# A first projection unit whose first 128 tokens are multiplied in fp32 from the loaded weights

## The reference

```
h = rms_norm(x, g_mix_pre)
proj = h @ w_in                       # q | k | v | u, 1024 columns each
attn = dilated_mixture_attention(q, k, v)
pool = multiscale_pool(u, w_pool, pool_scale)
x = x + rms_norm(concat(rms_norm(attn), rms_norm(pool)) @ w_out, g_mix_post)
x = x + rms_norm(square(relu(rms_norm(x, g_ffn_pre) @ w_up)) @ w_down, g_ffn_post)
```

## Time and profile before

| | us |
|---|---|
| median of 3 runs | 2038.19 |
| lowest and highest | 2036.93, 2038.52 |
| the profiled execution | 2039.06 |
| its span | 2037.3 |
| TensorE busy | 2018.1 |
| VectorE busy | 1228.1 |
| ScalarE busy | 930.5 |
| GpSimd busy | 122.1 |

### The profile page before, as it was taken

How to read it: one execution, slowest core, us unless ns; L and a number is a source line. 1 busy time by engine, 2 the same in 40 slices (tenths; PEclk the granted TensorE clock), 3 DMA queues, 4 the chain that set the end, 5 groups by cost and what they waited for, 6 DMA issues and landing times.

```text
span 2037.3 us, 29067 instructions
## 1 busy us (share of the span) xinstructions
PE 2018.1 (99%) x10042; PEld 1712.4 (84%) x10042; DVE 1228.1 (60%) x1386; ACT 930.5 (46%) x1224; POOL 122.1 (6%) x178
## 2 busy tenths in 40 slices
PE   8999999999999999999999999999999999999998
PEld 6888888888888888888888888888888888888886
DVE  5775657655665565565576646676556655655654
ACT  6445657434443443443564456563433443443442
POOL 1820011000000000000100000200000000000000
PEclk9999999999999999999999999999999999999999
DMA  7565355655665565665466543565565565566553
GB/s 269 166 217 170 118 177 175 200 203 168 201 206 169 194 197 184 207 201 190 165 218 199 182 155 134 176 196 187 189 200 189 180 205 189 171 209 212 174 199 132
DMA packets 196258, 380.57 MB, mean 187 GB/s; under 512 B 11888, under 2 KB 14048, under 8 KB 195552
## 3 DMA queue, kind: packets, MB, share of 16 engines
q1 hardware_dynamic: 196000, 379.15, 56.1%
q10 hardware_dynamic: 192, 0.54, 0.1%
HBM read 377.55 MB, written 2.10 MB: 186 GB/s over the span
## 4 chain that ended last, share of the span: by engine, by line
PE 94%; DMA 2%; DVE 2%; issue 1%; ACT 1%; POOL 0%; DVEq 0%; POOLq 0%; SPq 0%; ACTq 0%
PE acc_pair L451 24%; PE acc_pair L410 18%; PE acc_pair L412 18%; PE acc_pair L411 18%; PE acc_pair L455 12%; DMA raw<-in_w_in 1%; DVE w_lo L1049 1%; PE acc_pair L584 1%; PE acc_pair L545 1%; PE o_bank L613 1%; DVE h_both L1103 1%; DMA raw<-in_w_up 0%; ACT w_hi L744 0%; PE t_bank L595 0%; PE t_bank L570 0%
## 5 line engine op out<-in xcount | busy, mean ns | idle before, releaser
L1049 DVE TENSOR_TENSOR w_lo<-raw,w_hi 128x1024 fp32r<-128x1024 f32 x704 | 858.2, 1235 | 419.2 <-ACT w_hi L744 400.9
L744 ACT CAST w_hi<-raw 128x1024 fp32r<-128x1024 f32 x704 | 730.1, 1053 | 584.1 <-PE acc_pair L412 243.2
L451 PE MATMUL acc_pair<-h_both,w_hi 128*128 128x512 f32 x2176 | 548.1, 393 | 0.8 <-ACT proj L802 0.8
L410 PE MATMUL acc_pair<-w_hi,f_hi 128*128 128x512 f32 x1280 | 502.0, 392 | 0.0
L412 PE MATMUL acc_pair<-w_hi,f_lo 128*128 128x512 f32 x1280 | 498.4, 389 | 0.0
L411 PE MATMUL acc_pair<-w_lo,f_hi 128*128 128x512 f32 x1280 | 498.2, 389 | 0.0
L451 PEld LDWEIGHTS acc_pair<-h_both,w_hi 128*128 128x128 f32 x2176 | 391.0, 189 | 71.0 <-ACT proj L802 1.7
L455 PEld LDWEIGHTS acc_pair<-h_both,w_lo 128*128 128x128 f32 x2176 | 296.9, 190 | 21.2
L455 PE MATMUL acc_pair<-h_both,w_lo 128*128 128x256 f32 x2176 | 303.4, 282 | 0.0
L412 PEld LDWEIGHTS acc_pair<-w_hi,f_lo 128*128 128x128 f32 x1280 | 240.3, 188 | 50.2
L411 PEld LDWEIGHTS acc_pair<-w_lo,f_hi 128*128 128x128 f32 x1280 | 240.4, 188 | 49.1
(11 more groups left out here) (157 smaller groups left out, 738.1 us busy)
## 6 DMA issues: line engine op xcount, KB each, us to landing
raw<-in_w_up SPq DMA_DIRECT2D x256, 512.0 KB, 4.7
raw<-in_w_down SPq DMA_DIRECT2D x256, 512.0 KB, 4.8
raw<-in_w_in SPq DMA_DIRECT2D x128, 512.0 KB, 4.9
raw<-in_w_out SPq DMA_DIRECT2D x64, 512.0 KB, 5.1
w_pool_s<-in_w_pool SPq DMA_DIRECT2D x2, 1024.0 KB, 9.0
post_row<-in_g_mix_post SPq DMA_DIRECT2D x2, 1024.0 KB, 7.9
post_row<-in_g_ffn_post SPq DMA_DIRECT2D x2, 1024.0 KB, 7.5
out<-x SPq DMA_DIRECT2D x8, 256.0 KB, 2.3
```

Source lines behind the costliest of these rows:

```text
L410: pe.matmul(bank[:, :], xh, wh, start=begin and k == 0, stop=False)
L451: mm = pe.matmul(acc_pair[b][:, m, :], w_hi[:, slot, col:col + P], x_both.rearrange("p s n -> p (s n)"), start=begin and k == 0, stop=end ...
L744: act.copy(w_hi[:, half * PAIRS + p, :], raw[:, p, :]).then_inc(hi_made, 1)
L1049: dve.tensor_tensor(w_lo[:, slot, :], raw[:, p, :], w_hi[:, slot, :].bitcast(F32), ALU.subtract).then_inc(lo_made, 1)
```

## The change

For the first layer's first unit only:

- The first 128 tokens (`first_tokens`) are multiplied as 16 fp32 matmuls of 512 columns, from `h_f` (x turned and multiplied by the gain in fp32, by VectorE) and the loaded weights. It needs neither w_hi nor w_lo. The other 128 tokens (`second_tokens`) are multiplied as before, with `others_turn` ahead of their last pair.
- All eight pairs of weights are loaded without a wait, four into `raw` and four into `raw_b`. x is loaded in seven pieces. All these transfers are issued by SyncE, in the order in which they are needed. The loads of the second unit's first half wait for `lo_made` and for `raw_used`.
- `h_hi` of the first tokens becomes one copy for each piece on ScalarE, `h_lo` one subtraction on VectorE, in a new order among the casts and splits. h_hi and h_lo of the first tokens are still needed by later units.
- TensorE makes ten transposes of the identity ahead of the first gains and six behind the first turn of x, whose result isn't used.

```diff
-            load_half(w_in, 0, 0, 0, 0)
-            sp.dma_start(x[:, 1, :], x_rows[1]).then_inc(x_loaded[2], 16)
+            load_x(0, 0, c_cols(0))
+            load_first(0, 0)
+            load_x(1, 0, c_cols(1))
+            load_first(1, 0)
+            load_first(2, 0)
+            load_x(2, 0, c_cols(2))
+            load_first(3, 0)
+            load_first(0, 1)
+            load_x(3, 0, c_cols(3))
+            load_first(1, 1)
+            load_first(2, 1)
+            load_x(4, 1, c_cols(0))
+            load_first(3, 1)
+            load_x(5, 1, c_cols(1))
+            load_x(6, 1, slice(2 * CH, D))
...
+                    for p in range(PAIRS):
+                        sp.wait_ge(lo_made, RAW + p + 1)
+                        sp.wait_ge(raw_used, p + 1)
+                        sp.sem_inc(raw_loaded[p], 16)
+                        load_half(w_in, 0, 0, 3 * HALF_W, 2, (p,), False)
+                    load_half(w_in, 0, HALF_W, 3 * HALF_W, 3)
...
+            def idle_turns(n):
+
+                for j in range(n):
+                    pe.transpose(o_bank[:, h_cols(j % 4)], ident[:, :], ident[:, :])
+
             pe.wait_ge(ident_made, 2)
+            idle_turns(10)
             pe.wait_ge(gains_loaded, 16)
...
-            h_turns(0, 0, (0, 1))
+            h_turns(0, 0, (0,))
+            idle_turns(6)
...
+            def first_tokens():
+
+                pe.wait_ge(acc_free[0], 1)
+                for s in range(RING):
+                    half, p = s // PAIRS, s % PAIRS
+                    src, loaded = ((raw, raw_loaded), (raw_b, raw_b_loaded))[half]
+                    pe.wait_ge(loaded[p], 16)
+                    pe.wait_ge(h_f_ready, s // 2 + 1)
+                    for k in range(2):
+                        mm = pe.matmul(acc_bank[0][:, :], h_f[:, 2 * s + k, :],
+                                       src[:, p, c_cols(k)], start=(s, k) == (0, 0),
+                                       stop=(s, k) == (RING - 1, 1))
+                    if half == 0:
+                        mm.then_inc(raw_used, 1)
+                    if s in (0, 2, 4, 6):
+                        h_turns(0, 0, (s // 2 + 1,))
+                mm.then_inc(acc_done, 1)
+
+            def second_tokens():
+
+                h_turns(0, 0, (5,))
+                for half in range(2):
+                    for p in range(PAIRS):
+                        if (half, p) == (0, 1):
+                            h_turns(0, 0, (6, 7))
+                        if (half, p) == (1, 3):
+                            others_turn()
+                        pe.wait_ge(lo_made, half * PAIRS + p + 1 + RAW)
+                        pe.wait_ge(h_lo_made, h_pair(0, 0, 4 + 2 * half + p // 2) + p % 2 + 1)
+                        pair(1, p, half, half, h_hi, h_lo, 8 * half, acc_bank[1],
+                             half == 0, half == 1, 0)
...
+            def h_first(c):
+
+                dve.wait_ge(tb_done[c % 2], c // 2 + 1)
+                g = G_MIX + 4 * c
+                dve.tensor_tensor(h_f[:, 4 * c:4 * c + 4, :],
+                                  t_bank[c % 2][:, :].rearrange("p (k n) -> p k n", k=4),
+                                  gain[:, g:g + 4, None].to_broadcast([P, 4, P]), ALU.mult
+                                  ).then_inc(h_f_ready, 1)
...
+            h_first(0)
             split_lo(0, 0, (0,))
-            h_chunks(0, 0, (1,))
-            split_lo(0, 0, (1, 2, 3))
-            h_chunks(0, 0, (2,))
+            h_first(1)
+            split_lo(0, 0, (1,))
+            h_first_lo(0)
+            split_lo(0, 0, (2,))
+            h_first(2)
+            split_lo(0, 0, (3,))
+            h_first_lo(1)
             split_lo(1, 1, (0,))
-            h_chunks(0, 0, (3,))
+            h_first(3)
             split_lo(1, 1, (1,))
-            dve.wait_ge(x_loaded[2], 16)
+            h_first_lo(2)
+            h_first_lo(3)
+            for n in range(4):
+                dve.wait_ge(x_loaded[n], 16)
             dve.sem_inc(x_ready, 4)
             h_first_unit(0, 0, 0, False)
```

More of the change, by code:

```diff
@@ L194, in build @@
     junk = at("junk", [P, CH], F32, r_qkv + 4 * T * CH)
+    raw_b = at("raw_b", [P, RAW, 2 * CH], F32, r_acc)
+    h_f = at("h_f", [P, KT, P], F32, r_qkv + 8 * T * CH)
     act_f = at("act_f", [P, T, CH], F32, r_qkv)
@@ L243, in build @@
     ones_made, warm_done = sem("ones_made"), sem("warm_done")
-    x_loaded = [sem(f"x_loaded{n}") for n in range(3)]
+    x_loaded = [sem(f"x_loaded{n}") for n in range(7)]
     raw_loaded = [sem(f"raw_loaded{p}") for p in range(RAW)]
+    raw_b_loaded = [sem(f"raw_b_loaded{p}") for p in range(RAW)]
+    raw_used, h_f_ready = sem("raw_used"), sem("h_f_ready")
     pool_w_loaded = sem("pool_w_loaded")
@@ L312, in _, with load_x, load_first, load_half @@
             x_rows = x_in[0].rearrange("(t p) d -> t p d", p=P)
[L313 to L319, removed]
+            def load_x(n, t, cols):
+                sp.dma_start(x[:, t, cols], x_rows[t][:, cols]).then_inc(x_loaded[n], 16)
+            def load_first(p, half):
+                dst, loaded = ((raw, raw_loaded), (raw_b, raw_b_loaded))[half]
+                row = half * HALF_W + p * 2 * P
+                src = w_in[0:1, row:row + 2 * P, 0:CH]
+                sp.dma_start(dst[:, p, :].rearrange("p (k c) -> p k c", k=2),
+                             src.rearrange("a (k p) c -> p (a k) c", p=P)
+                             ).then_inc(loaded[p], 16)
+            def load_half(w, l, row, col, hu, which=range(PAIRS), held=True):
+                for p in which:
+                    if held:
+                        sp.wait_ge(lo_made, hu * PAIRS + p + 1)
                     src = w[ld(l, 1), ld(row + p * 2 * P, 2 * P), ld(col, CH)]
@@ L466, in h_turns @@
                     t, c = i // CHUNKS, i % CHUNKS
-                    pe.wait_ge(x_ready, l * 16 + 8 * h + i + 1)
-                    if i >= 2:
+                    if l or h:
+                        pe.wait_ge(x_ready, l * 16 + 8 * h + i + 1)
+                    else:
+                        pe.wait_ge(x_loaded[min(i, 6)], 16)
+                    if (l, h) == (0, 0) and i in (2, 3, 4, 5):
+                        pe.wait_ge(h_f_ready, i - 1)
+                    elif i >= 2:
                         pe.wait_ge(h_lo_made, h_pair(l, h, i - 1))
@@ L503, in others_turn @@
                              ).then_inc(gains_turned, 1)
+            def first_tokens():
[26 more added lines that the diff above has]
+                             half == 0, half == 1, 0)
+            first_tokens()
+            second_tokens()
             for l in range(DEPTH):
@@ L508, in _ @@
                 xg0 = XG_SLOTS + l * XG_LAYER
[L510 to L520, removed]
+                if l > 0:
+                    unit(hu0, a0, h_hi, h_lo, h_first_unit(l, 0))
                 def spread_rstd(n, p):
@@ L741, in split_hi @@
                 for p in which:
-                    act.wait_ge(raw_loaded[p], hu * 16 + 16)
+                    src = raw
+                    if isinstance(hu, int) and hu == 1:
+                        src = raw_b
+                        act.wait_ge(raw_b_loaded[p], 16)
+                    else:
+                        act.wait_ge(raw_loaded[p], hu * 16 + 16)
                     act.wait_ge(w_used, hu * PAIRS + p + 1)
-                    act.copy(w_hi[:, half * PAIRS + p, :], raw[:, p, :]).then_inc(hi_made, 1)
+                    act.copy(w_hi[:, half * PAIRS + p, :], src[:, p, :]).then_inc(hi_made, 1)
             def h_hi_pair(bank, g, dst):
@@ L1048, in split_lo @@
                     slot = half * PAIRS + p
-                    dve.tensor_tensor(w_lo[:, slot, :], raw[:, p, :],
+                    src = raw_b if isinstance(hu, int) and hu == 1 else raw
+                    dve.tensor_tensor(w_lo[:, slot, :], src[:, p, :],
                                       w_hi[:, slot, :].bitcast(F32), ALU.subtract
@@ L1140, in _, with h_first, h_first_lo @@
                             ).then_inc(gains_ready, 1)
-            dve.wait_ge(x_loaded[0], 16)
-            dve.sem_inc(x_ready, 2)
             dve.wait_ge(gain_ready, 1)
-            dve.wait_ge(x_loaded[1], 16)
-            dve.sem_inc(x_ready, 2)
-            h_chunks(0, 0, (0,))
-            split_lo(0, 0, (0,))
-            h_chunks(0, 0, (1,))
-            split_lo(0, 0, (1, 2, 3))
-            h_chunks(0, 0, (2,))
+            def h_first(c):
+                dve.wait_ge(tb_done[c % 2], c // 2 + 1)
[4 more added lines that the diff above has]
+                                  ).then_inc(h_f_ready, 1)
+            def h_first_lo(c):
+                dve.wait_ge(h_hi_made, 2 * c + 2)
+                part = slice(4 * c, 4 * c + 4)
+                dve.tensor_tensor(h_lo[:, part, h_cols(0)], h_f[:, part, :],
+                                  h_hi[:, part, h_cols(0)].bitcast(F32), ALU.subtract
+                                  ).then_inc(h_lo_made, 2)
+            h_first(0)
+            split_lo(0, 0, (0,))
```

(17 more changed lines are left out.)

16 lines of the change are left out of this document (8 added, 8 removed).

## The result

The changed kernel takes 2041.81 us (median of 19 runs, 2040.37 to 2042.82), the kernel before 2038.52 us in the same measurement. The ratio is 1.0015, 95% interval 1.0009 to 1.0022: 3.3 us slower, with a forecast of 3.8. The profiled execution took 2041.83 us with a span of 2040.0, 2.8 and 2.7 more than before.

The account below looks back on a forecast made before the run. TensorE, busy 99% of the span, was taken as the bound, with a nearly level path through VectorE. Plus 3.6 us for the late small gains and 0.2 for the clock gave plus 3.8: 2042.0 us, range 2039.6 to 2044.8.

Parts of the forecast that it names:

- The start: First matmul of the first unit: starts at 6.5 us instead of 10.59, 4.1 us sooner.
- third rival: First loads in one queue start slower, first weights landing at 8.1: plus 5.4 us, 2043.6; chance 0.1.
- The fp32 price: First tokens' fp32 matmuls: 0.87 us each, sixteen taking 13.9 us against 10.9 for 48 split ones, 3.0 more.
- VectorE's stall: Before the first split pair, TensorE waits from 22.6 to 24.7 us for VectorE's low part of h: 2.1 us.
- Turn 3: Turn of x in the first unit where VectorE's last stall starts; its end was forecast at 16.5 us.
- the path: From VectorE's wait through second-unit low parts, loads, casts, squares and root to the projection: TensorE resumes at 53.2 instead of 49.62.
- The deciding term: VectorE waits for the small gains' turn before the second unit's low parts: free at 35.5 instead of 31.89, 3.6 us later.
- The fourth rival: VectorE's wait for the small gains does not decide, so the kernel is not slower: 2034.9 us; chance 0.08.
- ledger of TensorE alone: TensorE's own work in the first unit: done at 34.6 instead of 37.95, so minus 3.3 us.
- The idle transposes: Assumed to raise TensorE's clock ahead of the first unit's matmuls, leaving a cost of only 0.2 us.
- second rival: Idle transposes leave the clock low until 10.2 us, losing 1.8 instead of 0.2: plus 5.4, 2043.6 us; chance 0.29.
- The stated bounds: Forecast case's start (6.2 or 7.3) and fp32 price move it by -0.5 to +1.1: 2041.2 to 2043.2 us.

Follow-up runs that it names:

- e7: Changed kernel with one swap in ScalarE's order, the cast of the sixth pair of weights ahead of the copy of the last piece of h: 2040.21 us.
- e1: Changed kernel with the turn of the small gains moved from ahead of the last split pair to ahead of the first: 2036.67 us.
- e3: Kernel before with only the turn of the small gains moved, to ahead of the last pair of the second tokens: 2042.99 us.
- e2: Changed kernel without the sixteen idle transposes, nothing else: 2043.32 us.
- e10: The changed kernel itself measured once more, in a later session: 2041.16 us.
- e4b: Kernel before with only the second half of the first tokens' x moved to SyncE's queue, behind the first pair of weights: 2038.70 us.
- e4: Kernel before with its first loads all on SyncE's queue and the first tokens' x in four pieces between the weights: 2039.94 us.
- e6: Changed kernel with its 10 + 6 idle transposes replaced by 5 + 3 idle fp32 matmuls of 128 columns: 2041.09 us.
- e9: The same kernel as e6 measured again, beside e10: 2042.02 us.
- e5: Changed kernel with the early cast of e7 and the early turn of the small gains of e1 together: 2036.39 us.

## Why the prediction was right

- **The start.** Forecast 6.5, found 6.67. The first piece of x landed at 0.73 + 3.70 = 4.43 (forecast 4.4), the first weights were cast from 6.03 on (forecast 6.2). The third rival, late loads, falls.
- **The fp32 price.** 3.44 us for four matmuls in the chain, 0.86 each, forecast 0.87, from twice the price at 256 columns. This term was right.
- **VectorE's stall.** TensorE's wait before the first split pair was forecast from 22.6 to 24.7 and found from 23.27 to 24.97. Turn 3 ended at 17.25 instead of 16.5, most of it since the low clock level cost 0.5 and not 0.2 and the start was 0.2 late. VectorE's steps from there to the first half of h took 7.6 us (17.25 to 24.87) and not 8.2, so the two errors nearly cancel. e7 shows that the stall was set by ScalarE's order and that it went down the path as stated.
- **The deciding term.** Gains turned at 35.50 (forecast 35.1), VectorE past them at 35.77 (35.5), TensorE back at 53.95 (53.2). e1 takes this wait away and wins 5.1 us; e3 puts it alone into the kernel before and loses 4.3. Together they show that this wait, and not the dearer matmuls, made the loss. The fourth rival falls. Its ledger of TensorE alone was sound: it gave minus 3.3 us, the stall makes that minus 1.7, and e1, where that ledger holds, is 2.0 under the kernel before.
- **The idle transposes.** The assumption that they raise the clock held: without them the low level cost 1.7 us and lasted until about 9.7 (forecast of the second rival: 1.8 us, until 10.2). But with them the clock did not come up shortly after 6.5: it cost 0.5 us in this profile where the sum has 0.2, and from nothing to 0.9 in the others. That e2's 1.5 us agree with the 1.6 between forecast and second rival is in part luck, since its trace shows 0.84 of them. The Trainium skill, "TensorE: Matmul & The Clock Gate", section "PE-mode transpose", speaks against the assumption; by e2's trace transposes do count here.
- **What was off.** One link of the path was mis-sized. The sum has VectorE 3.6 + 0.2 = 3.8 us late at the small gains, and it was 3.9. But the last load before the projection took 6.82 us where the 6.27 of the kernel before were carried over, so TensorE resumed 4.3 us late. Over the 13 profiles this load takes 5.4 to 6.8 us (6.82 and 6.52 in two of the changed kernel), and no run tells what sets it. With it the path closes in every profile where this path decides: the lateness of the load's issue plus the difference of its length gives TensorE's lateness within 0.02 us (e2 4.63 - 0.28 = 4.35, e3 4.87 + 0.10 = 4.97, e7 2.29 - 0.90 = 1.39, e10 3.76 + 0.25 = 4.01). The stated bounds do not follow either: minus 0.5 to plus 1.1 about 2042.0 is 2041.5 to 2043.1, and not 2041.2 to 2043.2.
- **What was luck.** The path says 4.3 us, the spans of the two profiles differ by 2.7, and the medians by 3.3. Between 204 us and the end 1.6 us were regained, which the forecast has nowhere; without them the time would have come out above its 3.8. TensorE's waits after 60 us, before:

```profile
PE acc_pair L410 <- DVE w_lo L1049: 1.6, 3, 0.6
PE acc_pair L451 <- ACT proj L802: 0.5, 1, 0.5
```

and after:

```profile
PE acc_pair L447 <- DVE w_lo L1134: 0.8, 2, 0.5
PE acc_pair L488 <- ACT proj L882: 0.2, 1, 0.2
```

That is 1.1 us of it. These waits stand where both kernels have the same work. In the twelve other profiles they come to 0.5 to 1.9 us without a pattern, and the 2.1 of the kernel before are the highest of all, in an execution 0.5 us above its median; so they belong to single executions. The other 0.5 us stay open.

## What to carry to other kernels

When a start is made faster, look for the small things that were placed beside the old order: a turn of 80 columns that had 7 us in hand became the one thing on which the next unit's weights waited, and moving it turned a loss of 3.3 us into a gain of 2. Where two paths come level (here 0.34 us apart), work out what each is worth after the change before counting what is saved on one. Weights that land sooner bring nothing while the engines ask for something else first: in the kernel before they landed 1.45 us sooner (e4b) and 2.15 us sooner (e4), and no time was won.

## What the runs showed of the hardware

- A fp32 matmul of 512 columns costs 0.86 us in a stream, as two records of 0.43; the three split matmuls that it replaces cost 0.68.
- The granted clock of the windows reads 1.00 where the spacing of matmuls shows the 1.2 GHz level. The packed trace's list of the granted clock begins only with the rise, at 14.41 us in the kernel before, and a stretch without an entry counts as full speed. At the start of a kernel the spacing, or the start of that list, is what to read.
- The point at which the clock rises differs between executions of one kernel: 5.18 and 7.47 us for e6 and e9, 5.59 and 7.68 for two profiles of the changed kernel. What the low level costs the first four records with idle work ahead goes from nothing (1.89 us in e1) to 0.9 us (2.74 in e5).
- The load of 512 KB that ends before the projection takes 5.4 to 6.8 us from issue to landing, with the same loads issued around it; no run tells why.
